# High and low activations in one 512-column matmul, two matmuls per weight block in place of three

## The reference

```
u = rms_norm(h, norm1_g);  proj = u @ w_in                   # q, k, v, z
mixed = concat([dilated_attention(q, k, v), rwkv7_time_mix(z)])
h = h + mixed @ w_out
gate, up = split(rms_norm(h, norm2_g) @ w_gate_up)
h = h + (silu(gate) * up) @ w_down;  x = rms_norm(h, final_g)

proj = rms_norm(x) @ w_in_2 + b_in_2
x = x + concat([conv_group(...), swa_group(...)]) @ w_out_2
xn = rms_norm(x);  experts, gates = top16 of (xn @ peer_w_q) against peer_sub_keys
h = xn . peer_u[experts];  a = gelu(h) * gates
x = x + sum(a * peer_v[experts])
```

## Time and profile before

| | us |
|---|---|
| median of 3 runs | 3692.64 |
| the runs | 3686.79 to 3694.71 |
| the profiled execution, device time | 3677.1 |
| its span from first to last instruction | 3675.2 |
| PE busy | 3387.9 (92%) |
| POOL busy | 2494.5 (68%) |
| DVE busy | 1525.4 (42%) |
| ACT busy | 1492.4 (41%) |

### The profile page before, as it was taken

The page is one execution under the profiler, slowest core; times in us unless marked ns, Lnnn a source line. Parts: engine busy times, 40 slices in busy tenths (PEclk is TensorE's granted clock), DMA queues, the critical chain, the costliest instruction groups (busy, mean ns, idle before and its releaser), DMA issues.

```text
span 3675.2 us, 74921 instructions
## 1 busy us (share of the span) xinstructions
PE 3387.9 (92%) x29214; PEld 3301.6 (90%) x29214; DVE 1525.4 (42%) x2484; ACT 1492.4 (41%) x1968; POOL 2494.5 (68%) x1079
## 2 busy tenths in 40 slices
PE   7899977689999999978768999999999999999999
PEld 6787767679999999977768999999999999999999
DVE  2057555532222210057961086666660266116600
ACT  4345533234444433344434455334344334433333
POOL 5664510268888878845436878777788777877787
PEclk9998989799999999988889999999999999999999
DMA  5843300246555656633324556555556555655555
GB/s 173 190 133 115 115 25 3 86 131 183 181 182 182 182 168 193 194 116 114 93 67 145 178 160 182 161 171 155 171 161 189 175 172 164 184 175 171 171 172 170
DMA packets 158600, 556.40 MB, mean 151 GB/s; under 512 B 17504, under 2 KB 23840, under 8 KB 158352
## 3 DMA queue, kind: packets, MB, share of 16 engines
q1 hardware_dynamic: 151008, 540.08, 48.4%
q0 software_dynamic: 2704, 9.25, 1.4%
q10 hardware_dynamic: 4768, 5.36, 0.5%
HBM read 549.38 MB, written 5.24 MB: 151 GB/s over the span
## 4 chain that ended last, share of the span: by engine, by line
PE 82%; DVE 11%; issue 3%; ACT 1%; POOL 1%; DMA 1%; POOLq 0%; ACTq 0%; DVEq 0%; SPq 0%
PE ps L528 73%; DVE ps L1627 2%; PE ps L715 2%; PE ps L584 1%; PE ps L901 1%; POOL wl L472 1%; PE ps L545 1%; DMA raw<-w_qkv 1%; DVE arena L1596 1%; DVE ul L1493 1%; DVE misc L1594 0%; DVE arena L1480 0%; DVE under_ul L1298 0%; DVE el L1762 0%; DVE arena L1424 0%
## 5 line engine op out<-in xcount | busy, mean ns | idle before, releaser
L472 POOL TENSOR_TENSOR wl<-raw,wh 128x1024 fp32r<-128x1024 f32 (+1 forms) x1034 | 2471.3, 2396 | 1081.7 <-ACT wh L975 1081.5
L975 ACT ACTIVATE wh<-raw 128x1024 fp32r<-128x1024 f32 (+1 forms) x1034 | 1086.2, 1052 | 1723.1 <-PE ps L528 1663.7
L528 PE MATMUL ps<-uh,wh 128*128 128x256 f32 x5584 | 1619.8, 290 | 112.5 <-DVE ul L1311 43.9
L528 PE MATMUL ps<-ul,wh 128*128 128x256 f32 x5584 | 1604.6, 287 | 0.0
L528 PE MATMUL ps<-uh,wl 128*128 128x256 f32 x5584 | 1603.9, 287 | 0.0
L528 PEld LDWEIGHTS ps<-uh,wh 128*128 128x128 f32 x5584 | 1099.1, 197 | 128.7 <-DVE ul L1311 45.5
L528 PEld LDWEIGHTS ps<-ul,wh 128*128 128x128 f32 x5584 | 1098.5, 197 | 0.5
L528 PEld LDWEIGHTS ps<-uh,wl 128*128 128x128 f32 x5584 | 1098.0, 197 | 0.0
L528 PE MATMUL ps<-el,wh 128*128 128x256 f32 x2048 | 574.2, 280 | 0.0
L528 PE MATMUL ps<-eh,wh 128*128 128x256 f32 x1536 | 439.7, 286 | 9.2 <-DVE el L1762 5.6
L528 PE MATMUL ps<-eh,wl 128*128 128x256 f32 x1536 | 430.2, 280 | 0.0
(11 more groups left out here) (312 smaller groups left out, 3030.3 us busy)
## 6 DMA issues: line engine op xcount, KB each, us to landing
raw<-w_u SPq DMA_DIRECT2D x256, 512.0 KB, 3.6
raw<-w_v SPq DMA_DIRECT2D x256, 512.0 KB, 3.6
raw<-w_gu SPq DMA_DIRECT2D x176, 512.0 KB, 3.6
raw<-w_down SPq DMA_DIRECT2D x80, 512.0 KB, 3.7
raw<-w_out SPq DMA_DIRECT2D x64, 512.0 KB, 3.6
raw<-w_z SPq DMA_DIRECT2D x54, 512.0 KB, 3.6
raw<-w_in SPq DMA_DIRECT2D x52, 512.0 KB, 3.6
raw<-w_qkv SPq DMA_DIRECT2D x48, 512.0 KB, 3.7
```

The source lines that it names most:

```text
L472: pool.tensor_tensor(wl[:, slot, 0:width], raw[:, slot, 0:width], wh[:, slot, 0:width].bitcast(F32), ALU.subtract).then_inc(lo_ready, 1)
L528: ins = pe.matmul(out, w[:, slot, at], x(c), start=first and c == n == 0, stop=last and c == kt - 1 and n == 2)
L975: act.activation(wh[:, slot, 0:width], raw[:, slot, 0:width], ACT.Copy).then_inc(hi_ready, 1)
```

## The change

The high and low activations now lie in one tensor (`uhl`, `ghl`, `ehl`), so that one access pattern reaches both halves. A new `pair_unit` streams [high | low], 512 columns, past `wh` into the whole bank, and the high part alone, 256 columns, past `wl` into the bank's first half: two matmuls per block. The bank then holds two partial sums, which are added when it is emptied. New helpers are `pair_tile` (two units) and `add_halves` (a DVE reduction of 512 columns to 256).

Which stages: the q and k part of qkv (32 units), gu (176), down (96 units, 704 blocks), out2 (32), wq (32), u2, u3, v0, v1 and v2 (64 each). The v part of qkv, z, out, in2, u0, u1 and v3 keep `unit`.

Who adds the halves: in qkv and wq, DVE with `add_halves` in place of ACT's copy (`take_sums`). In gu, DVE with `add_halves` for the gate bank into `GS` and for the up bank into bank 4 or 5; the product and its two parts are then taken from there. In down, out2 and v0 to v2, two additions to `xT` in place of one. In u2 and u3, DVE with `add_halves` into banks 4 to 7, from which ACT takes gelu; the lows of the quarter before are made between the first four sums.

```
+            def pair_unit(b, ready, slot, pair, k0, kt=UKT, first=True, last=True):
+                pe.wait_ge(lo_ready, ready)
+                for c in range(kt):
+                    at = slice(c * P, (c + 1) * P)
+                    pe.matmul(bank(b).rearrange("p (n t) -> p n t", n=2), wh[:, slot, at], pair[:, :, k0 + c, :],
+                              start=first and c == 0, stop=False, skip_group_check=True)
+                    ins = pe.matmul(bank(b)[:, 0:T], wl[:, slot, at], pair[:, 0, k0 + c, :], start=False,
+                                    stop=last and c == kt - 1, skip_group_check=True)
+                return ins
...
             def gate_up(i, first):
                 for j in range(4):
                     if not first:
-                        pe.wait_ge(gp_ready, i * 2 + (j // 2 - 1))
-                    tile(bank(j)[:, 0:T], i * 8 + (g0 + 2 * j), (g0 + 2 * j) % RING, uhc, ulc,
-                         (u_ready, 2 * DT) if first and j == 0 else None)
+                        pe.wait_ge(up_sum, i * 2 + (j // 2 - 1))
...
+                        pair_unit(j, i * 8 + (g + 1), g % RING, UHL, UKT * n, first=n == 0, last=n == 1)\
+                            .then_inc(w_used, 1)
...
             def experts_in(q, i, first=False, turn=None):
...
-                        pe.wait_ge(u_ev, i * 4 + (QJ * q + j - 1))
+                        pe.wait_ge(*((u_ev, i * 4 + (QJ * q + j - 1)) if q < 2 else
+                                     (exp_sum, i * 4 + (QJ * (q - 2) + j - 1))))
...
+            def add_halves(out, b):
+                return dve.tensor_reduce(out, bank(b).rearrange("p (n t) -> p t n", n=2), AX, ALU.add)
...
+            def take_sums(out, name, done):
+                with dve.Fori(0, DT // 2) as i:
+                    for j in range(2):
+                        dve.wait_ge(w_used, i * 4 + (BASE[name] + 2 * j + 2))
+                        add_halves(out[:, bass.ds(i * 2 + j, 1), :].rearrange("p a t -> p (a t)"), j)\
+                            .then_inc(done, 1)
...
                     dve.wait_ge(w_used, i * (2 * DOWN_U) + (BASE["down"] + DOWN_U * (j + 1)))
-                    dve.tensor_tensor(xT[:, bass.ds(i * 2 + j, 1), :], xT[:, bass.ds(i * 2 + j, 1), :],
-                                      ps[:, j:j + 1, 0:T], ALU.add).then_inc(res_ready, 1)
+                    x = xT[:, bass.ds(i * 2 + j, 1), :]
+                    dve.tensor_tensor(x, x, ps[:, j:j + 1, T:2 * T], ALU.add).then_inc(res_low, 1)
+                    dve.wait_ge(res_low, i * 2 + (j + 1))
+                    dve.tensor_tensor(x, x, ps[:, j:j + 1, 0:T], ALU.add).then_inc(res_ready, 1)
...
+            def sum_experts(q, i, lows_of=None):
+                for j in range(4):
+                    dve.wait_ge(w_used, i * 8 + (BASE[f"u{q}"] + 2 * j + 2))
+                    dve.wait_ge(u_ev, i * 4 + (QJ * q + j - 3))
+                    add_halves(bank(4 + j)[:, 0:T], j % 2).then_inc(exp_sum, 1)
+                    if lows_of is not None:
+                        expert_low(lows_of, 2 * j)
+                        expert_low(lows_of, 2 * j + 1)
```

More of the change, by code:

```diff
@@ L530, in unit, with pair_tile @@
                 return ins
+            def pair_unit(b, ready, slot, pair, k0, kt=UKT, first=True, last=True):
[7 more added lines that the diff above has]
+                return ins
+            def pair_tile(b, g, pair, second=None):
+                for n in range(2):
+                    if n and second:
+                        pe.wait_ge(*second)
+                    pair_unit(b, g + (n + 1), (g + n) % RING, pair, UKT * n, first=n == 0, last=n == 1)\
+                        .then_inc(w_used, 1)
             def tile(out, g, slot, xh, xl, second=None):
@@ L555, in loop @@
                         pe.wait_ge(evac, i * 4 + (before + at + j - 1))
-                        tile(bank((at + j) % 2)[:, 0:T], i * 8 + (g0 + 2 * j), (g0 + 2 * j) % RING, uhc, ulc)
+                        for n in range(2):
+                            g = g0 + 2 * j + n
+                            pair_unit((at + j) % 2, i * 8 + (g + 1), g % RING, UHL, UKT * n, first=n == 0, last=n == 1)\
+                                .then_inc(w_used, 1)
             uhc = lambda c: uh[:, c, :]
@@ L569, in _ @@
                     pe.wait_ge(qkv_ev, j - 1)
-                tile(bank(j % 2)[:, 0:T], 2 * j, 2 * j % RING, uhc, ulc, None if j else (u_ready, DT))
+                pair_tile(j % 2, 2 * j, UHL, None if j else (u_ready, DT))
             loop("qkv", 4, 12, qkv_ev, 0)
@@ L876, in _ @@
                     pe.wait_ge(res_ready, 2 * DT + c - 1)
-                tile(bank(c % 2)[:, 0:T], g, g % RING, lambda c: uh[:, (c + WT) % DT, :],
-                     lambda c: ul[:, (c + WT) % DT, :], None if c else (ml_ready, 2 + WT + 4))
+                for n in range(2):
+                    if c == 0 and n:
+                        pe.wait_ge(ml_ready, 2 + WT + 4)
+                    pair_unit(c % 2, g + (n + 1), (g + n) % RING, UHL, WT * (1 - n), first=n == 0, last=n == 1)\
+                        .then_inc(w_used, 1)
             norm_sum(4, mix2)
@@ L884, in _ @@
                     pe.wait_ge(wq_ev, j - 1)
-                tile(bank(j % 2)[:, 0:T], g, g % RING, uhc, ulc, None if j else (u_ready, 5 * DT))
+                pair_tile(j % 2, g, UHL, None if j else (u_ready, 5 * DT))
             loop("wq", 4, 12, wq_ev, 0)
@@ L951, in _ @@
                 pe.wait_ge(res_ready, (2 + q) * DT)
-                with pe.Fori(0, 8) as i:
+                experts_in(q, 0, first=True)
+                with pe.Fori(1, 8) as i:
                     experts_in(q, i)
@@ L1789, in _ @@
                 add_out(q, 7, True)
[L1790 to L1791 removed]
+                if q + 2 < NQ:
+                    sum_experts(q + 2, 0, lows_of=q + 1)
+                    with dve.Fori(1, QJ // 4) as i:
+                        sum_experts(q + 2, i)
+                elif q < NQ - 1:
+                    for k in range(8):
+                        expert_low(q + 1, k)
 def units(w):
```

113 lines of the change are left out of this document (70 added, 43 removed).

## The result

The changed kernel takes **3647.2 us** (median of 4 runs, 3645.7 to 3652.5) where the kernel before takes 3692.4: ratio 0.988, 95% interval 0.9865 to 0.9899. It is faster by 45 us; the forecast was 112 us faster, and the time lies 2 us above its range. The profiled execution has a span of 3643.8 us (before 3675.2).

The account below looks back on a forecast made before the run. TensorE's time per weight block was taken to bound the kernel. 117 us won by pairs, less 5 at stage ends, is 112 off the median of 3692.6: 3581 us, range 3520 to 3645.

Parts of the forecast that it names:

- What bounds the kernel: Dense stages: TensorE's time per weight block decides; the feed has room until that time falls by more than a tenth.
- That it gets faster: Whole kernel: a third of the matmuls and loads goes in changed blocks, winning only surpluses; faster had chance 0.80.
- The pitch of the long matmul: Paired blocks: a 512-column matmul takes 215.2 ns, 1.9 above its columns, as in the norm's plain fp32 records.
- the load outlasts the matmul: Before each 256-column matmul the array waits for a load of about 110 ns, which a long matmul hides.
- The pitches of the stages: Time per 256-column matmul, kept for the short one: 120.1 ns in gu and u, 113.3 in down, 117.8 in v.
- rival (a): Every matmul, long or short, carries the same surplus; a gu pair is 320 ns and two surpluses; 3635 us, chance 26%.
- the 5 us for stage ends: Longer TensorE waits where stages end, 3.8 us, plus 1 for stretches at half clock; bounds 0 and 15.
- The difference between profile and median: The profiled execution of the kernel before ran 15.5 us quicker than its median; this was carried over to the forecast.
- Beside TensorE: Sums of halves on DVE (0.69 us each) and second additions cost nothing, covered by TensorE's work; uncovered, reductions cost 127 us.
- (b): Paired blocks: with fewer loads both matmuls run at their columns, 323.8 ns per pair; 3527 us, chance 13%.
- (c): No gain: the surplus is a rate per column, or the chip splits a 512-column matmul in two; 3687 us, chance 11%.
- rival (d): Slower: the two-part moving operand goes at a worse pace; 3761 us, over 1 ms lost at plain fp32's pace; chance 9%.

Follow-up runs that it names:

- experiment 4: Changed kernel with the long matmul split into two of 256 columns, each with its own load, halves still summed: 3688.1 us, 0.9987 of the kernel before.

## Why the prediction was wrong

**What bounds the kernel** was right: TensorE's time per block decides, and POOL and the DMAs followed. **That it gets faster** was right too: a matmul with its load falls away, and with it a surplus.

**The pitch of the long matmul, 215.2 ns, is the step that failed**; it is about 232 in gu and 227.4 alone. It was taken from the plain fp32 records of the earlier trace rows, which have 1.9 ns over 213.3, while this kind has 13.3 over its columns at 256, 320 and 384 and 14.1 at 512. The row was near in time and far in kind: its records are of 256 columns, and two of them make one matmul, so 430 ns are the pace of 256 plain fp32 columns and not of 512, as rival (d) has it. Nothing in the forecast's sum hangs on that. The reading behind it, that the load outlasts the matmul and hides once the matmul is long, was half right at most: short matmuls don't come closer than 111.7 ns, near the 110 read for a load, but the surplus stays where the matmul is longer than that. Rows 3, no surplus at half clock, fitted both. The Trainium skill (TensorE: Matmul & The Clock Gate, Back-to-back issue gap) gives 2.5 ns over the columns as the gap of a matmul by itself, by an estimate from it 215.8 ns for 512, and about 131 ns per 512-column matmul for a stream of loads and matmuls. The 227.4 ns measured here, with a load for each, agree with neither.

**The pitches of the stages, 120.1, 113.3 and 117.8, were read as properties of the stages**; that step failed as well, and it is why rival (a), right about gu to 0.1 ns (346.8), still misses with 3635. Down's 113.3 was the level of one execution, and the pair there got 353.3 where (a) has 333.2.

In the profiled executions the forecast missed by 81 us of span (3563 against 3643.8). By the terms: 3200 blocks at 13.3 gained in place of 25.0 are 37 us, 704 at 13.4 lost in place of 11.4 gained 17, 1536 at 3.0 in place of 20.4 27: 81 us. z, with unchanged code, took 6 us more; the 5 us for stage ends were not spent, and down began at full clock; these about cancel. **z's 6 us stay open**: up to the stage behind it z had 451.6 and 451.3 us in the two profiles of the changed kernel and 445.1 in both of the kernel before, but also 451.5 in the one with everything moved, which has no pair. Most of it is waiting: over z's own blocks TensorE is idle for 29.0 us in the changed kernel and 23.5 in the one before. What shifts these waits wasn't shown.

**The difference between profile and median was carried over, 15.5 us**; the changed kernel's was 1.5. The first profile of the kernel before had down at 340.0, 9 us less than in its second, so part of those 15.5 us was the level and no offset. That the one profile read had this level was luck.

**Beside TensorE** the operations were as costed, and experiment 4 bears out that the sums of halves are free. Of the waits at stage ends, forecast 0.8 us longer into v1 and 0.5 into u3 and 1 us shorter into down, the first did not grow and the others moved by 0.2 and 1.5 us. The rivals: (b), 323.8 ns, is excluded, since no stretch of either form was below 340.0. (c) and (d) didn't come, though (c)'s end, no gain from the pair, is what well placed operands give. I took the pair's gain to be one of form, and what the change harvests is open to three matmuls as well, by moving the weights 64 bytes.

## What to carry to other kernels

A time per matmul that is read from one profile may be a level and no property of the stage: profile twice, and read a stage whose code is the same in both kernels. Before matmuls are restructured for the gaps between them, try where weights and activations lie modulo 256 bytes; that costs a pad and moved this kernel by 2 to 2.6%, more than the change itself (1.2%). Price a new shape by a small kernel of the same kind of operand, since a row of another type can be off by the whole effect.

## What the runs showed of the hardware

- At full clock an fp32r matmul with its own 128-wide load, activations and weights at the same place, took its columns and 13.3 ns at 256, 320 and 384 columns and 14.1 at 512; in threes of 256 columns it was 6.7 ns with 64- and 32-wide loads, or at a good place. At half clock there was none.
- With 128 and 192 columns it took 111.7 ns.
- The time per block goes in levels, mostly 6.7 ns apart. Which are open depends on the places of activations against weights modulo 256 bytes; which one is taken, on the start, and it is kept until the next stop, of which 0.30 us was enough. In threes, moving all by 64 bytes changed nothing, moving the weights alone took 20 ns off a block (360.0 to 340.0) and moving the activations alone 6.7.
- Down began at half clock after a wait of 4.12 us and at full clock after one of 2.64; v1, after the same 1.80 us, at full clock in one profile and at half clock in the other.
- What in TensorE makes the levels wasn't shown, nor why stages with other matmuls between their blocks (u1, v0 to v2) take another one than dense stages at the same place.
